# A decoder block in fp32 on one core: sixteen expert rows move into the last product, and unsplit units are shared out anew

## What is computed

```python
h = rms_norm(x, g_pre_ffn) * (1.0 + sc_f) + sh_f
q = (h @ w_q)                                   # 2048 x 2048
s1, s2 = q[..., :128] @ k1.T, q[..., 128:] @ k2.T   # 8 heads, 128 keys each
cand = top16(s1) + top16(s2); idx = top16(cand); g = softmax(top)
u, vv = u_tab[idx], v_tab[idx]                  # two tables, 16384 rows of 2048
act = gelu(einsum('thkd,td->thk', u, h)) * g
ff = einsum('thk,thkd->td', act, vv)
x = x + gt_f * rms_norm(ff, g_post_ffn)
```

## Time and profile before

| | |
|---|---|
| median of three runs | 1789.8 us |
| the profiled execution | 1789.97 us, its span 1788.1 us |
| TensorE busy in matmuls | 1753.1 us, 98% |
| VectorE busy | 1518.6 us, 85% |
| ScalarE busy | 792.1 us, 44% |
| GpSimd busy | 584.4 us, 33% |
| DMA | 617.22 MB, mean 345 GB/s |

### The profile page before, as it was taken

One profiled execution on the slowest core, in us unless ns is written; L12 is line 12 of the kernel. 1 busy time (PEld: TensorE's weight loads), 2 busy tenths in 40 slices (PEclk: granted clock), 3 DMA queues, 4 the chain that ended last, 5 costly groups with the idle time before them and its releaser, 6 DMA issues.

```text
span 1788.1 us, 27779 instructions
## 1 busy us (share of the span) xinstructions
PE 1753.1 (98%) x9548; PEld 1529.8 (86%) x9548; DVE 1518.6 (85%) x2445; ACT 792.1 (44%) x1155; POOL 584.4 (33%) x388
## 2 busy tenths in 40 slices
PE   7999999999999999989999999999999999999998
PEld 6888888544999999989999999998888888888885
DVE  4668899967677999889998899989888888888887
ACT  3001222401645666433455555555545545554554
POOL 1000000011000288788878878722111111111110
PEclk9999999999999999999999999999999999999999
DMA  9999976799686677889999999999999999999994
GB/s 382 420 420 423 422 298 256 259 418 399 264 333 257 194 212 217 302 278 322 326 392 391 395 386 405 402 373 403 373 373 355 380 359 373 369 372 364 369 375 197
DMA packets 123724, 617.22 MB, mean 345 GB/s; under 512 B 42851, under 2 KB 43395, under 8 KB 52099
## 3 DMA queue, kind: packets, MB, share of 16 engines
q1 hardware_dynamic: 64258, 426.81, 61.5%
q0 software_dynamic: 53056, 184.69, 29.3%
q10 hardware_dynamic: 6338, 4.80, 0.8%
HBM read 599.22 MB, written 16.88 MB: 345 GB/s over the span
## 4 chain that ended last, share of the span: by engine, by line
PE 76%; DMA 9%; DVE 8%; issue 4%; POOL 2%; ACT 1%; DVEq 0%; SPq 0%; ACTq 0%
PE ps L1357 32%; PE ps L1026 13%; PE ps L1033 8%; PE ps L1193 5%; PE ps L1077 5%; DMA raw<-in_w_ada 5%; PE ps L1247 4%; PE ps L1019 2%; PE ps L1088 2%; POOL weights L528 2%; DVE raw L1456 1%; DMA early<-in_w_front 1%; DVE w_low L1398 1%; DMA big<-in_w_gate_f 1%; DVE big L1512 1%
## 5 line engine op out<-in xcount | busy, mean ns | idle before, releaser
L735 ACT ACTIVATE w_hi<-raw 128x1024 fp32r<-128x1024 f32 x512 | 542.4, 1060 | 486.8 <-PE ps L1357 238.1
L1398 DVE TENSOR_TENSOR w_low<-raw,w_hi 128x1024 fp32r<-128x1024 f32 x512 | 623.8, 1224 | 118.0 <-ACT w_hi L735 109.7
L528 POOL DMA_INDIRECT weights<-sel x192 | 370.3, 1929 | 239.3 <-DVE sel L1832 181.1
L1357 PE MATMUL ps<-w_hi,a 128*128 128x512 f32 x1536 | 390.0, 389 | 2.1 <-ACT big L834 1.5
L1026 PE MATMUL ps<-a,w_hi 128*128 128x384 f32 x1792 | 360.1, 342 | 0.8 <-issue 0.8
L1357 PEld LDWEIGHTS ps<-w_hi,a 128*128 128x128 f32 x1536 | 288.1, 188 | 62.6 <-ACT big L834 1.7
L1026 PEld LDWEIGHTS ps<-a,w_hi 128*128 128x128 f32 x1792 | 306.0, 189 | 1.6 <-issue 1.6
L1357 PE MATMUL ps<-w_low,a 128*128 128x512 f32 x1024 | 274.0, 389 | 0.0
L1033 PEld LDWEIGHTS ps<-a,w_low 128*128 128x128 f32 x1792 | 229.3, 191 | 13.7 <-DVE w_low L1398 12.9
L1033 PE MATMUL ps<-a,w_low 128*128 128x192 f32 x1792 | 233.5, 272 | 7.3 <-DVE w_low L1398 6.8
L1357 PEld LDWEIGHTS ps<-w_low,a 128*128 128x128 f32 x1024 | 192.0, 188 | 40.5 <-DVE w_low L1398 0.7
(11 more groups left out here) (227 smaller groups left out, 1804.6 us busy)
## 6 DMA issues: line engine op xcount, KB each, us to landing
raw<-in_peer_u SPq DMA_DIRECT2D x128, 1024.0 KB, 6.9
raw<-in_peer_v SPq DMA_DIRECT2D x128, 1024.0 KB, 7.0
early<-in_w_front SPq DMA_DIRECT2D x56, 1024.0 KB, 11.6
raw<-in_w_ada POOLq DMA_DIRECT2D x48, 1024.0 KB, 9.7
raw<-in_w_ada SPq DMA_DIRECT2D x32, 1024.0 KB, 12.6
raw<-in_peer_wq SPq DMA_DIRECT2D x16, 1024.0 KB, 4.8
big<-in_w_gate_f SPq DMA_DIRECT2D x16, 1024.0 KB, 7.0
weights<-third SPq DMA_DIRECT2D x16, 768.0 KB, 19.1
```

The lines of the kernel that those rows point to most:

```text
L528: gp.indirect_dma_start(weight_elements, bass.IndirectOffsetOnAxis(ap=put_at[:, c:c + 1], axis=0), put_gate[:, c:c + 1], None, compute_op= ...
L735: act.activation(w_hi[:, h % 2, :], raw[:, s % RING, :], ACT.Copy).then_inc(hi_ready, 1)
L1357: done = pe.matmul(ps[:, 4 * tt + 2 * (j % 2) + n, :], a, w[:, n * 512:(n + 1) * 512], start=i is None and blk == 0 and m in (0, 2), stop= ...
L1398: dve.tensor_tensor(w_low[:, s % RING, :], raw[:, s % RING, :], w_hi[:, h % 2, :].bitcast(F32), ALU.subtract).then_inc(lo_ready, 1)
```

## The change

- MID's unsplit units go from eight of 16 to two (7 and 15), UP gets the same two. That is eight each in place of 0 and 32.
- No dots in MID. The 16 rows taken out are gathered and multiplied in turns 1 to 8 of DOWN, two to a turn, into one buffer; there the v rows have two buffers in place of four. From turn 9 on DOWN is as before. `acc` lies elsewhere to make room.
- GpSimd runs 84 puts behind the first three gathers, then two behind each of the next 28.
- `by_vector` holds for THIRD too.
- The first four chunks of the query's first pass are unsplit, and computed for tile 0 while tile 1 is not ready; the idle products are gone.
- GELU of the dots is taken in two parts (48 and 16 columns), the second between turns 8 and 9.

```diff
-PH_WQ = Phase(None, BLOCKS // 4, 8)
-PH_UP = Phase(PH_WQ, EXPERT_BLOCKS // 32, 16, groups=tuple(range(22, 30)))
-PH_MID = Phase(PH_UP, EXPERT_BLOCKS // 32, 16, plain=(1, 3, 5, 7, 9, 11, 13, 15), groups=(30, 31, 4, 11, 12, 13, 14, 15))
+FIRST_PLAIN = 4
+PH_Q0 = Phase(None, 1, 8, plain=tuple(range(FIRST_PLAIN)))
+PH_WQ = Phase(PH_Q0, BLOCKS // 4 - 1, 8)
+PH_UP = Phase(PH_WQ, EXPERT_BLOCKS // 32, 16, plain=(7, 15), groups=tuple(range(22, 30)))
+PH_MID = Phase(PH_UP, EXPERT_BLOCKS // 32, 16, plain=(7, 15), groups=(30, 31, 4, 11, 12, 13, 14, 15))
...
-FOUR_ROWS, SIX_ROWS = (1, 2, 5, 6, 9, 10, 13, 14), (0, 1, 3, 4, 5, 6, 8, 9, 11, 12, 13, 14)
-DOTS = {PH_MID: (tuple(range(8, 16)), FOUR_ROWS), PH_THIRD: (SIX_ROWS, SIX_ROWS), PH_LAST: (SIX_ROWS, SIX_ROWS)}
+SIX_ROWS, TWO_ROWS, LATE_STEPS = (0, 1, 3, 4, 5, 6, 8, 9, 11, 12, 13, 14), (1, 3, 9, 11), 8
+DOTS = {PH_THIRD: (SIX_ROWS, SIX_ROWS), PH_LAST: (SIX_ROWS, SIX_ROWS), PH_DOWN: ((), TWO_ROWS)}
...
-PUTS_BEHIND = [0] + [4, 4, 3] * 5 + [2, 2, 2, 2, 1] * 10
+PUTS_BEHIND = [0, 0, 84] + [2] * 28
...
+def v_buffer(step, m):
+
+    return (0, 2)[m % 2] if step <= LATE_STEPS else m
...
-            return ph is PH_DOWN or ph is PH_LAST and (n >= 0 or i is not None)
+            return ph in (PH_LAST, PH_DOWN) or ph is PH_THIRD and (n >= 0 or i is not None)
...
-            for n in range(ROWS):
+            for n in range(EARLY_ROWS):
                 if ROW_NTH[n] > 1:
                     gp.wait_ge(row_used, max(m for m in range(n) if ROW_BUF[m] == ROW_BUF[n]) + 1)
...
+            free = [(row_used, EARLY_ROWS - 2), (row_used, EARLY_ROWS - 1), (split_used, PH_DOWN.s), (row_used, ROWS)]
+            def late_row(n):
+                gp.wait_ge(*free[1])
+                gather(n, u_rows, got[1], row_in[3])
+                free[1] = (row_used, n + 1)
+            def v_row(step, m):
+                b, n = v_buffer(step, m), V_PER * step + m
+                if n == 1:
                     gp.wait_ge(at_made, 1)
+                gp.wait_ge(*free[b])
+                gather(n, v_rows, got[b], v_row_in[b])
+                free[b] = (v_row_used, n + 1)
+            for step in range(V_STEPS):
+                for m in range(V_PER):
+                    v_row(step, m)
+                    if m % 2 == 0 and 1 <= step <= LATE_STEPS:
+                        late_row(EARLY_ROWS + 2 * (step - 1) + m // 2)
...
-            for k in range(4):
-                turn_x2(k, 0)
-            keep_going(ps[:, MIX_FIRST[3], 2 * P:3 * P], 26)
-            pe.wait_ge(x2_diag, 2)
+            for k in range(FIRST_PLAIN):
+                turn_x2(k, 0).then_inc(turned_first, 1)
+            for k in range(FIRST_PLAIN):
+                if k % 2 == 0:
+                    pe.wait_ge(landed[k // 2], 16)
+                pe.wait_ge(h_first, k + 1)
+                plain_query(k, 0, range(4))
             pe.wait_ge(mix_sq, 8)
             pe.wait_ge(mix_gated, 8)
+            for k in range(FIRST_PLAIN):
+                plain_query(k, 0, range(4, 8))
+            pe.wait_ge(x2_diag, 2)
+            for k in range(FIRST_PLAIN):
+                turn_x2(k, 1).then_inc(turned, 1)
...
-            act.wait_ge(dots_put, N_DOT_STEPS)
-            act.activation(dots[:, :], dots[:, :], ACT.Gelu).then_inc(row_gelu, 1)
+            row_gelus(N_DOT_STEPS - LATE_STEPS, slice(0, EARLY_ROWS))
             down(None)
-            with act.Fori(1, PH_DOWN.n - 1) as i:
+            with act.Fori(1, LATE_STEPS + 1) as i:
+                down(i)
+            row_gelus(N_DOT_STEPS, slice(EARLY_ROWS, ROWS))
+            with act.Fori(LATE_STEPS + 1, PH_DOWN.n - 1) as i:
                 down(i)
```

More of the change, by code:

```diff
@@ L105 @@
     DOT_ROWS[ph], DOT_STEPS[ph] = first, steps if peeled else steps - 1
-    first += len(peeled) // 2 + (ph.n - 1) * len(looped) // 2
-    steps += (len(peeled) > 0) + ph.n - 1
+    times = LATE_STEPS if ph is PH_DOWN else ph.n - 1
+    first += len(peeled) // 2 + times * len(looped) // 2
+    steps += (len(peeled) > 0) + times
 N_DOT_STEPS = steps
 assert first == ROWS
-THREE_FROM = DOT_ROWS[PH_THIRD]
-ROW_BUF = [n % 2 if n < THREE_FROM else (2, 0, 1)[(n - THREE_FROM) % 3] for n in range(ROWS)]
+EARLY_ROWS = DOT_ROWS[PH_DOWN]
+ROW_BUF = [n % 3 if n < EARLY_ROWS else 3 for n in range(ROWS)]
 ROW_NTH = [ROW_BUF[:n + 1].count(ROW_BUF[n]) for n in range(ROWS)]
@@ L117 @@
 PUTS_UP = 52
-PUTS_BEHIND = [0] + [4, 4, 3] * 5 + [2, 2, 2, 2, 1] * 10
-PUTS_AT = [min(PUTS_UP + sum(PUTS_BEHIND[:n]), PUTS) for n in range(ROWS + 1)]
-assert PUTS_AT[ROWS] == PUTS
+PUTS_BEHIND = [0, 0, 84] + [2] * 28
+PUTS_AT = [min(PUTS_UP + sum(PUTS_BEHIND[:n]), PUTS) for n in range(EARLY_ROWS + 1)]
+assert PUTS_AT[EARLY_ROWS] == PUTS
+V_STEPS, V_PER = PH_DOWN.n, ROWS // PH_DOWN.n
+def v_buffer(step, m):
+    return (0, 2)[m % 2] if step <= LATE_STEPS else m
 SUMS_FIRST, SUMS_AT = (6, 8, 9, 10, 12, 13, 14, 15), (0, 2, 4, 6, 8, 10, 12, 14)
@@ L326, in build_block @@
         picked_ready, row_info_in = sem("picked_ready"), sem("row_info_in")
-        row_in = [sem(f"row_in{n}") for n in range(3)]
+        row_in = [sem(f"row_in{n}") for n in range(4)]
         v_row_in = [sem(f"v_row_in{n}") for n in range(4)]
@@ L782, in high_chunk @@
                 act.activation(a_hi[:, k, :], h_full[:, k, :], ACT.Copy).then_inc(h_hi, 1)
-            high_chunk(0)
-            high_chunk(1)
-            for u in range(2, KC):
+            for k in range(FIRST_PLAIN):
+                high_chunk(k)
+            wq_hi(FIRST_PLAIN)
+            high_chunk(FIRST_PLAIN)
+            for u in range(FIRST_PLAIN + 1, KC):
                 high_chunk(u)
@@ L1401, in lo @@
                     sum_block(ph, j // 2 - 1, i)
-                if ph in DOTS:
+                if ph in DOTS and ph is not PH_DOWN:
                     dots_at(ph, j, i)
@@ L1427, in dots_at @@
                         dve.wait_ge(dots_put, at(i, 1, steps))
-                here = (got[0], got[1], third)[buf][:, cols]
+                here = (got[0], got[1], third, got[1])[buf][:, cols]
                 d = dve.tensor_tensor_reduce(here, here, h_tok[:, cols], 1.0, 0.0, ALU.mult,
@@ L1717, in low_chunk @@
                     .then_inc(h_ready, 1)
[L1719 to L1722 removed]
+            for k in range(FIRST_PLAIN):
+                low_chunk(k)
+            for u in range(FIRST_PLAIN, KC):
+                wq_lo(u)
                 low_chunk(u)
[L1724 to L1726 removed]
+                gate_f_step(u - 4)
             for u in range(KC, 2 * KC):
@@ L1884, in low_group, with down @@
                                   a_down[:, b:b + 4, 2 * P:P + TD].bitcast(F32), ALU.subtract).then_inc(at_lo, 1)
-            def down(i, last=False):
+            def down(i, rows=False, last=False):
                 for j in range(PH_DOWN.per):
```

136 lines of the change are left out of this document (80 added, 56 removed).

## The result

The changed kernel takes 1821.45 us, the median of four executions (1815.99 to 1823.62). The kernel before, on the same chip, takes 1789.88 (1789.32 to 1790.97). The ratio is 1.0174, with a 95% interval of 1.0162 to 1.0187: slower by 31.6 us, where the prediction said 13, and 2.5 us above its range. The profiled execution took 1823.62 us, its span 1821.8, which is 33.7 more than the span before.

The account below looks back on a forecast made before the run. TensorE's products plus stalls were taken to bound each stage. Terms -26.8 (query, UP, MID, THIRD), +27.5, +1.5, +5 and +7 gave +14.2 on 1789.97, 1804.2 us; 1803 was forecast, range 1779 to 1819.

Parts of the forecast that it names:

- The bound and the gains: All stages: each lasts as long as TensorE's products plus stalls; UP was to change by -2.8 us, MID by -15.6.
- THIRD's sums: THIRD: no product with the identity in 31 blocks, 0.11 us each, -3.5 us; VectorE's extra sums cost nothing.
- Query: Query's first pass: unsplit chunks, tile 0's computed while tile 1 is not ready, -4.9 us, between 0 and -5.6.
- GpSimd's order: THIRD's first turn: 84 puts at 2.13 us delay the fourth u row's gather to 904.8 us, stalling TensorE, +27.5 us.
- the gap: THIRD, unit 9: TensorE wants it at 889.3 us and gets it at 916.8, a stall of 27.5 us.
- The clock: THIRD, after the stall: TensorE runs partly at 1.2 GHz, costing +1.5 us.
- drift: Behind the stall: a row costs GpSimd 6.4 us against TensorE's 6.12, over 27 rows, +5 us, 0 to 7.
- UP's price: Cost of a put: 2.19 us in UP, from which 2.13 was taken for MID with two subtractions fewer.
- DOWN: DOWN: turns 1 to 8 take 36.9 us against 36.36, plus late v row and second GELU, +7 us, 0 to +21.
- The rival that reached +21: DOWN bound by its rows: DMA gives 400 GB/s or rows land late, 38.7 us a turn, 1818 us; chance 0.15.
- Turn 1: DOWN's first turn: with two buffers a v row is asked for too late, +2 us.
- The term of 36.7 us: DOWN, turns 1 to 8: DMA carries 15.5 MB a turn at 421 GB/s, the most a long stretch shows.

Follow-up runs that it names:

- the run with 89: The changed kernel with 89 puts instead of 84 behind the third row's gather and five fewer behind the last rows: 1826.84 us.
- the run without gathers: The changed kernel without gathering the 16 late u rows in DOWN, their dot products still running on what stands in the buffer: 1817.94 us.
- both repairs: The changed kernel with 66 puts instead of 84 behind the first three gathers, the rest redistributed, and ScalarE's `high_group` one unit later in DOWN: 1779.78 us.
- three buffers: The kernel with both repairs, and in DOWN's turn 0 the third v row placed in the buffer that late u rows use later: 1776.65 us.
- without the late gathers: The kernel with both repairs and three buffers, without gathering the 16 late u rows, their dot products still running: 1769.48 us.
- short dots: The changed kernel with DOWN's dot products taken over 16 columns instead of 1024, rows still gathered: 1807.38 us.
- `high_group` moved: The changed kernel with ScalarE's `high_group` one unit later in DOWN, behind unit 6 of a half turn instead of 5: 1810.22 us.

## Why the prediction was too low

**The bound and the gains: right.** Reading a stage as its products plus its stalls gave UP and MID within 0.6 us. MID's stalls went with its rows. THIRD's sums are worth 3.5 us where they take effect, as forecast; at the end of the kernel before, 1.8 of it arrive.

**Query: right in its parts, not in its sum.** An unsplit chunk with its turn takes 2.24 us (453.23 to 455.47), as worked out, and the fifth chunk comes 3.5 us earlier (462.09 against 465.55), since tile 0's part ends at 451.85 and the turns come behind it. The pause at 499.64 costs 1.45 more.

**GpSimd's order: the mechanism right, three sizes wrong that cancel.** The gather came 0.4 us from its forecast, and the 84 puts ahead of it cost 2.14 us each for 2.13 (724.24 to 904.42). That mean hides two prices: 2.18 for the 76 puts up to 889.59, while VectorE works, and 1.85 for the eight in the stall. But TensorE wanted unit 9's low products at 912.56 - 18.79 = 893.8, 4.5 us later than forecast, mostly because the query had gained less, and the row landed in 5.7 us (904.42 to 910.14), not 9.7, with DMA busy 0.72 of that stretch. So the gap was 18.8 for 27.5. The clock cost 3.0 for 1.5: two units took 4.44 and 3.15 us from start to start, in place of 2.29. Behind it 64 units took 159.0 us (959.13 to 1118.10), where 16 undisturbed ones take 36.69: that is 12.2 us of drift for 5. A row cost GpSimd 6.51 us (17 gathers, 979.16 to 1083.33) for the forecast 6.4, against TensorE's 6.12. Together 34.0 for 34. That the sum came out is luck: 8.7 us too much for the gap, 8.7 too little for the clock and the drift. The distribution of the puts is confirmed as the cause by the run that changed nothing else and took 32.1 us off.

The rule of the Trainium skill, "SBUF — State Buffer", Who interferes with whom, counted as the prediction did, had the put at 2.09; the 84 puts took 2.14, so the forecast from UP's price was the better one. What the rule says of the mechanism is borne out by the ten puts ahead of 912.61 in the run with 89: VectorE idle, 1.85 each.

**DOWN: the step that failed.** The prediction took VectorE's busy time, 32.0 of 36.36 us, and added 4.9 to it, as if all its idle time were free: "So in turns 1 to 8 three resources have the same length, and I take 36.9". Of the 4.4 idle us in a turn 2 x 0.83 are a wait inside the chain VectorE, ScalarE, VectorE, and they don't shrink when VectorE gets more to do. VectorE is busy 36.36 us of a turn now (181.78 in the five turns from 1303.5), which would nearly have fitted under TensorE's 36.27 and is 0.5 less than the 36.9 of the forecast; with 1.67 of wait and 0.15 of short gaps that is 38.18. It stood in the trace of before, 0.83 us at 1403.98, hidden by TensorE. The rival that reached +21 had the right size for another reason, DMA, and the run without gathers rules that reason out. The prediction gave it 0.15. Of the 15.7 us that the forecast of DOWN was short, 9.4 are these seven turns (1.9 each for 0.55); most of the rest is turn 1.

**Turn 1** was +2 in the forecast, of a v row asked for too late. Its v and u rows together cost 5.4 us of waits (3.13 and 2.28), and the turn 9.1. The runs take it apart one after the other: 45.73 in the changed kernel, 44.16 with both repairs, 40.94 with three buffers, 38.68 without the late gathers, against 36.59 before. So the loop has 1.6 us of it, the v rows' two buffers 3.2 and the late u rows 2.3. The last 2.1 are work: VectorE is busy 34.11 us in turn 1 of the kernel before (1219.35 to 1255.94) and not 32.0, and 38.52 of the 38.68. The forecast took the mean of later turns for this one too, and put the u row's wait at nothing.

**DMA.** The term of 36.7 us, 15.5 MB at 421 GB/s, was right as a floor: 36.76 with the short dots, where DMA was the bound. By the Trainium skill, "DMA: Bandwidth & Descriptors", Specifications, at 435 GB/s it would be an estimated 35.6 and no floor at all; the trace disagrees, since no slice of 45 us in the pages of the profiles here passes 424.

## What to carry to other kernels

An engine's idle time is spare only as far as it isn't a wait for an engine that in turn waits for it: before work is moved onto the second busiest engine, read what ends its gaps, and subtract the gaps whose releaser stands behind this engine's own output. Such a loop may be mended for nothing, by putting the quick link of the chain one place later in its queue. And where one queue serves two purposes, shortening the stages ahead of it brings its deadline forward and not its work: move the order in the queue with the change.

## What was not expected of the hardware

- A gather of 1 MB issued in the stall, with DMA busy 0.72 (904.42 to 910.14), landed in 5.7 us; in the full stream of the kernel before the median is 9.7.
- Steady streams together stop at 417 to 424 GB/s with a share of 1.01 or 1.02, gathers of rows among them or not. With puts among them it is less at a share that is no lower: 357 to 382 GB/s at 1.01 to 1.05 (960 to 1080 us of the changed kernel).
- TensorE's lower clock after 18.8 us of idle time cost 3.0 us, and after 27.9 us 2.8 (units of 4.43 and 2.94 us). After the gap of 18.6 to 18.7 us in three more of the kernels it was 1.8 (`high_group` moved), 2.8 (no late gathers) and 1.7 (short dots). So the price scatters between 1.7 and 3.0, and it did not grow with the length of the gap.
- A put, with the pause behind it, costs GpSimd 2.18 us while VectorE works and 1.85 while VectorE stands still.
